# A decoder step in three-pass fp32: the cached keys of the samples scored by products and sums instead of transposes and matmuls

## The reference, cut to what matters

```python
def _dilated_step(q, k, v, buf, window, dil):
    ...
    nk = window // dil + 1                       # 129: 128 cached rows and the sample's own
    g = kv[:, jnp.maximum(cidx, 0)]
    s = jnp.einsum('bthe,btjhe->bthj', q, g[:, :, :, 0])
    lse = jax.nn.logsumexp(s, axis=-1)
    p = jnp.exp(s - lse[..., None])
    o = jnp.einsum('bthj,btjhe->bthe', p, g[:, :, :, 1])
    return o, lse, kv[:, T:]
```

## Time and profile before

| what | value |
|---|---|
| median of 3 runs | 911.78 us (911.31 to 916.65) |
| profiled execution, its own time | 912.07 us |
| its span, first to last instruction | 910.3 us |
| TensorE busy | 900.8 us (99%) |
| VectorE, ScalarE, GpSimd busy | 66%, 54%, 24% |
| bytes moved by DMA | 281.18 MB, mean 309 GB/s |

### The profile page before, as it was taken

The page is one execution under the profiler, slowest core; times in us unless marked ns, Lnnn a source line. Parts: engine busy times, 40 slices in busy tenths (PEclk is TensorE's granted clock), DMA queues, the critical chain, the costliest instruction groups (busy, mean ns, idle before and its releaser), DMA issues.

```text
span 910.3 us, 19532 instructions
## 1 busy us (share of the span) xinstructions
PE 900.8 (99%) x7987; PEld 868.7 (95%) x7987; DVE 601.5 (66%) x868; ACT 488.6 (54%) x753; POOL 216.1 (24%) x233
## 2 busy tenths in 40 slices
PE   8999999999999999999999999999999999999998
PEld 8999999999999999999999999789999999999998
DVE  6666665659975688797887544355548666666543
ACT  6444434445545677677866455246675644443332
POOL 0433330005710000069871113000001043333000
PEclk9999999999999999999999999999999999999999
DMA  9988969999987877789988688849999799998971
GB/s 353 401 309 310 321 227 340 334 356 379 329 306 259 322 255 271 287 316 408 416 316 286 235 267 254 295 163 351 336 367 343 267 352 376 374 364 287 353 221 48
DMA packets 62440, 281.18 MB, mean 309 GB/s; under 512 B 8176, under 2 KB 9328, under 8 KB 60624
## 3 DMA queue, kind: packets, MB, share of 16 engines
q1 hardware_dynamic: 23328, 148.32, 42.9%
q10 hardware_dynamic: 39024, 131.61, 42.5%
HBM read 256.65 MB, written 111.32 MB: 404 GB/s over the span
## 4 chain that ended last, share of the span: by engine, by line
PE 91%; DVE 3%; ACT 2%; DMA 1%; issue 1%; POOL 1%; SPq 0%; ACTq 0%; DVEq 0%; POOLq 0%
PE acc L427 16%; PE acc L428 15%; PE acc L429 15%; PE att L427 11%; PE att L428 10%; PE att L429 10%; PE aux L1063 2%; DVE wl L407 1%; PE att L1188 1%; PE att L1122 1%; DMA kv<-cache 1%; ACT wh L401 1%; PE att L805 1%; PE aux L1027 1%; PE att L1258 1%
## 5 line engine op out<-in xcount | busy, mean ns | idle before, releaser
L407 DVE TENSOR_TENSOR wl<-raw,wh 128x1024 fp32r<-128x1024 f32 (+2 forms) x280 | 334.3, 1196 | 219.5 <-ACT wh L401 214.5
L401 ACT ACTIVATE wh<-raw 128x1024 fp32r<-128x1024 f32 (+2 forms) x280 | 277.0, 994 | 186.8 <-PE acc L429 104.0
L427 PE MATMUL acc<-hh,wh 128*128 128x264 f32 x496 | 145.8, 294 | 0.1
L428 PE MATMUL acc<-hl,wh 128*128 128x264 f32 x496 | 140.8, 284 | 0.0
L429 PE MATMUL acc<-hh,wl 128*128 128x264 f32 x496 | 140.6, 284 | 0.0
L427 PE MATMUL acc<-xh,wh 128*128 128x264 f32 x416 | 118.7, 285 | 1.7 <-DVE wl L407 1.7
L427 PE MATMUL att<-xh,wh 128*128 128x264 f32 x416 | 118.5, 285 | 0.3 <-DVE xl L532 0.3
L428 PE MATMUL acc<-xl,wh 128*128 128x264 f32 x416 | 117.8, 283 | 0.0
L428 PE MATMUL att<-xl,wh 128*128 128x264 f32 x416 | 117.8, 283 | 0.0
L429 PE MATMUL att<-xh,wl 128*128 128x264 f32 x416 | 117.8, 283 | 0.0
L429 PE MATMUL acc<-xh,wl 128*128 128x264 f32 x416 | 117.8, 283 | 0.0
(11 more groups left out here) (264 smaller groups left out, 2075.2 us busy)
## 6 DMA issues: line engine op xcount, KB each, us to landing
raw<-w ACTq DMA_DIRECT2D x207, 512.0 KB, 6.9
state<-state_in SPq DMA_DIRECT2D x32, 512.0 KB, 9.1
state_out<-state SPq DMA_DIRECT2D x32, 512.0 KB, 6.0
raw<-w ACTq DMA_DIRECT2D x32, 384.0 KB, 5.9
kv<-cache SPq DMA_DIRECT2D x48, 256.0 KB, 4.5
raw<-w ACTq DMA_DIRECT2D x32, 320.0 KB, 5.5
raw<-w SPq DMA_DIRECT2D x9, 512.0 KB, 9.0
kv_out<-cache SPq DMA_DIRECT2D x3, 960.0 KB, 7.2
```

Source lines behind the costliest of these rows:

```text
L401: nc.scalar.activation(wh[n % HI_RING][:, 0:slot_size(n)], raw[n % RAW_RING][:, 0:slot_size(n)], ACT.Copy).then_inc(hi_done, 1)
L407: nc.vector.tensor_tensor(wl[n % RAW_RING][:, 0:slot_size(n)], raw[n % RAW_RING][:, 0:slot_size(n)], wh[n % HI_RING][:, 0:slot_size(n)].bi ...
L427: nc.tensor.matmul(out, w_hi, xh, start=first, stop=False)
L428: nc.tensor.matmul(out, w_hi, xl, start=False, stop=False)
```

## The change

The scores of the cached keys leave TensorE. There are now six **items** (two halves of four samples x three groups). An item's keys are loaded as two buffers of 128 partitions x 2 rows x 512, with four cache rows of a sample on each partition. The queries are packed by GpSimd, transposed once by TensorE (`pe_q_rows`, v11), and for each item VectorE spreads its query row over the partitions with a stream shuffle (`dve_key_spread`, 128 x 512 from PSUM). The keys are multiplied by the spread query in place, 128 x 1024 at a time: item 0 on VectorE, items 1 to 5 on GpSimd (`key_product`). VectorE sums each product over the 64 numbers of a head (`dve_key_sum`, 128 x 1024 to 128 x 16). The softmax is made for four samples at a time along the free axis after a VectorE transpose; the three groups are joined by shuffles between partitions. The values come as 12 more buffers in eight loads of 128 KB an item; `pe_dec_v` has the same 24 matmuls of 512 columns, now in slots 9, 11, 16 and 17. Turn, gather and output are done twice, once for each half of the samples. `split_ob` on GpSimd comes after item 1's products, and TensorE waits for its parts one by one in slots 0 and 1. The two transposes of an item of the prompt's attention share one bank.

Elsewhere: slots 0 and 1 of the kernel are rounded in halves, and gate A is read from PSUM with tanh(x/2) in the ga slots, so that the eight sigmoids fall away; the merge becomes (tanh + 1) * A * 0.5 + B in the same two VectorE instructions a tile.

```diff
+        ITEMS = 2 * G
+        ON_POOL = (1, 2, 3, 4, 5)
...
+        def dve_key_spread(dve, i):
+            if i == 0:
+                dve.wait_ge(q_rows, 1)
+            if i >= 2:
+                dve.wait_ge(key_mul, (2, 4, 8, 10)[i - 2])
+            c, g = i // G, i % G
+            nc.vector.stream_shuffle(spread_buffer(i)[:], bank6[:], [2 * g + c] * 32).then_inc(key_spread, 1)
+
+        def key_product(eng, ops, i, half):
+            eng.wait_ge(kv_in[i % 3], kv_landed(i))
+            eng.wait_ge(key_spread, i + 1)
+            if i:
+                eng.wait_ge(key_mul, 2 * i + half)
+            elif half:
+                eng.wait_ge(key_mul, 1)
+            keys = kv_buffer(i, half)
+            ops.tensor_tensor(keys[:], keys[:], spread_buffer(i)[:].unsqueeze(1).to_broadcast([P, 2, AW]),
+                              ALU.mult).then_inc(key_mul, 1)
+
+        def dve_key_sum(dve, i, half):
+            dve.wait_ge(key_mul, 2 * i + half + 1)
...
+            nc.vector.tensor_reduce(to, kv_buffer(i, half)[:].rearrange("p k (h e) -> p k h e", h=AH), AX.X,
+                                    ALU.add).then_inc(key_sum, 1)
...
+        def pe_own_score(pe):
...
+            for t in range(AT):
+                a = 2 * (AT - 1 - t)
+                for j in range(4):
+                    last = nc.tensor.matmul(bank7[32 * j:32 * j + 32, 0:2], head[:, a:a + 32], own_prod[:, t, j:B:4],
+                                            start=t == 0, stop=t == AT - 1)
...
-        DEC_V = {2: (7,), 3: (4, 4), 4: (5,), 5: (5, 5)}
-        OA_SPLIT = {0: (0,), 1: (1,), 3: (2,), 6: (3,)}
+        DEC_TURN = {6: 0, 14: 1}
+        DEC_V = {9: (0, 1), 11: (2,), 16: (3, 4), 17: (5,)}
+        DEC_GATHER = {13: 0, 19: 1}
+        KEY_SPREAD = {-8: 0, -7: 1, -4: 2, -1: 3, 4: 4, 6: 5}
+        KEY_PRODUCT = {-6: (0,), -5: (1,)}
+        KEY_SUM = {-6: (0,), -5: (1,), -3: (2,), -2: (3,), 0: (4,), 1: (5,), 3: (6,), 4: (7,), 6: (8, 9), 8: (10, 11)}
+        SOFT_MAX = {1: 0, 9: 1}
+        SOFT_EXP = {2: 0, 10: 1}
+        SOFT_SUM = {3: 0, 11: 1}
+        OWN_ROWS = {12: 0, 18: 1}
+        DEC_OUT = {13: 0, 19: 1}
+        OA_SPLIT = {4: (0,), 5: (1, 2), 6: (3,)}
...
-                nc.scalar.activation(gate_a[:, t], acc[bank_of(p_ga, t)][:, 0:T], ACT.Copy).then_inc(out_of["act"], 1)
+                nc.scalar.activation(gate_a[:, t], acc[bank_of(p_ga, t)][:, 0:T], ACT.Tanh, scale=0.5).then_inc(out_of["act"], 1)
...
-            for m in range(KD):
-                nc.scalar.activation(gate_a[:, m], gate_a[:, m], ACT.Sigmoid).then_inc(gate_done, 1)
...
-            for h in range(RH):
-                split_ob(h)
+            pool_pad(pool)
+            for i in range(ITEMS):
+                if i == 2:
+                    for h in range(RH):
+                        split_ob(h)
+                for half in range(2):
+                    if i in ON_POOL:
+                        pool_key_product(pool, i, half)
...
+                    if m == 0 and k % 4 == 0:
+                        pe.wait_ge(ob_split, k // 4 + 1)
```

More of the change, by code:

```diff
@@ new lines, in kv_landed, with sp_kv_load @@
+        def kv_landed(n):
+            return sum(32 if m < ITEMS else 128 for m in range(n % 3, n + 1, 3))
+        def sp_kv_load(sp, n):
+            if n >= 3:
+                kv_used(sp, n - 3)
+            c, g = n % ITEMS // G, n % G
+            dil = GROUPS[g][1]
+            for half in range(2):
+                buffer = kv_buffer(n, half)
+                if n < ITEMS:
+                    rows = caches[g][4 * c:4 * c + 4].rearrange("b w c -> (b w) c").rearrange(
+                        "(p k d) c -> p k d c", k=4, d=dil)
+                    sp.dma_start(buffer[:], rows[:, 2 * half:2 * half + 2, 0, 0:AW]).then_inc(kv_in[n % 3], 16)
+                else:
+                    two = caches[g][4 * c + 2 * half:4 * c + 2 * half + 2].rearrange("b (p k d) c -> k p b d c", k=4, d=dil)
+                    for k in range(4):
+                        sp.dma_start(buffer[32 * k:32 * k + 32], two[k, :, :, 0, AW:2 * AW]).then_inc(kv_in[n % 3], 16)
@@ new lines, in pe_dec_v @@
+        def pe_dec_v(pe, i):
+            c, g = i // G, i % G
+            if g == 0:
+                pe.wait_ge(dec_act, 2 * c + 2)
+            n = ITEMS + i
+            pe.wait_ge(kv_in[n % 3], kv_landed(n))
+            for j in range(4):
+                a = 32 * j + AH * g
+                last = nc.tensor.matmul(bank7[32 * j:32 * j + 32, :], dec_pT[:, a:a + 32], kv_buffer(n, j // 2)[:, j % 2],
+                                        start=g == 0, stop=g == G - 1)
+            last.then_inc(dec_v_done, 1)
@@ L1290, in pe_own_score @@
-        def pe_own_score(pe):
-            for g in range(G):
-                for n in range(4):
-                    last = nc.tensor.matmul(bank7[32 * n:32 * n + 16, G * P + g:G * P + g + 1], own_blk[:, 4 * g + n],
-                                            ones[:, 0:1], start=False, stop=g == G - 1, skip_group_check=True)
-            last.then_inc(dec_pe, 1)
-        NK = G * P + G
-        def dve_dec_max(dve):
-            dve.wait_ge(dec_pe, 1)
-            nc.vector.tensor_reduce(dec_m[:, 0:1], bank7[:, 0:NK], AX.X, ALU.max).then_inc(dec_dve, 1)
-            dve.wait_ge(dec_dve, 1)
-            nc.vector.tensor_scalar(dec_m[:, 1:2], dec_m[:, 0:1], -SCALE, None, ALU.mult).then_inc(dec_dve, 1)
@@ L1493, in _ @@
             sp.wait_ge(qk_done, AT)
[L1494 to L1503 removed]
+            for n in range(2 * ITEMS):
+                sp_kv_load(sp, n)
             for q in range(p_pb.q0 + 2, fi2.q0):
@@ L1841, in _ @@
                     dve_v_tile(dve, p_v, AT - V_LAST + t)
-                for i in range(3 * t, 3 * t + 3):
-                    if i % 2:
-                        key_copy(dve, i)
+                dec_steps(t - KD)
                 if t == 1:
```

470 lines of the change are left out of this document (232 added, 238 removed).

## The result

The changed kernel takes 920.5 us (median of 5 runs, 919.5 to 922.9), the kernel before 912.5 in the same comparison: ratio 1.0089, 95% interval 1.0073 to 1.0106. The forecast was 904, with a range of 892 to 914. The profiled execution after has a span of 919.4 us and took 921.22; the one before, 912.07. So there are 9.15 us to explain between the two profiles, and 17 between forecast and profile.

What follows compares the result with a forecast made beforehand. TensorE's own queue was taken as the bound (busy 900.8 of 910.3 us at full clock). From 912.1 us, a gross gain of 20.8 less 13 of stalls gave 904.3, about 904; own range 900 to 908, full range 892 to 914.

Steps and rivals of the forecast that it cites:

- Costs that I put at nothing: Key and value loads and SyncE's delayed cache rolls: a few bunched, covered by ten slots of weights, no cost.
- The clock: TensorE's granted clock might fall in the stalls, making the forecast wrong; no case in the old trace, no size given.
- the stalls: VectorE and GpSimd excluding each other, and VectorE's order, make TensorE wait: 16.0 us laid out, 13 taken, bounds 3 and 16.
- The gross gain: Work off TensorE 18.2, start 1.0, gate 1.2 and small waits 0.4: 20.8 us before stalls.
- The own scores: On TensorE, 96 passes with 32 weight columns and 2 moving ones: 1.6 us added, bounds 1.2 and 2.4.
- The two small changes: First weight tiles in halves gain 1.0 us (bounds 0, 1.6); gate without sigmoids gains 1.2 (bounds 0, 1.3).
- slot 5, for its weights: Item 2's sums, a softmax and blocked low parts make slot 5's weights ready at 572.7, not 571.1: 1.6 us.
- `prob`, first: VectorE reaches the attention's first scores at 582.0, division ends 584.65, TensorE is there at 580.2: 4.5 us lost.
- `prob`, second: Slot 6's spread and two sums stand before the other half's reciprocal on VectorE: 3.4 us lost.
- B: Rival: engines overlap better because GpSimd runs in the gaps; stalls 4 us, time 895 us; chance 0.33.
- C: Rival: GpSimd's in-place product with broadcast input costs 5.2 us, not 2.4, adding 25; time 929 us; chance 0.09.
- D: Rival: stalls reach all 16 us and a few late loads or restarts add to them; time 910 us; chance 0.13.

Runs made afterwards that it cites:

- e1_paced: Changed kernel with SyncE's list of cache rolls begun at slot 12, not slot 8, also called the paced kernel; 909.9 us, ratio to before 0.9967.
- e5_small_packets: Changed kernel with its heap of rolls kept, each roll issued as two transfers in 2 KB pieces; 910.0 us, ratio to before 0.9965.
- e3_no_products: e1_paced with all twelve key products left out, so scores are not the reference's; 896.8 us, ratio to before 0.9821.
- e6_small_two: Kernel before with only the first two weight tiles prepared in halves and the gate by tanh; 911.5 us, ratio 0.9987.
- e7_behind: e1_paced with VectorE's cached-key steps put behind the attention's own steps from slot 5 on; 905.5 us, ratio to before 0.9917.
- e11_sum_later: e9_one_spread_later plus item 1's products on VectorE and TensorE's small retention sum at the end of g0; 904.8 us, ratio to before 0.9920.
- The five arrangements: Five variants of e1_paced moving steps between slots, engines or order, nothing left out; 905.5, 917.2, 906.4, 905.5 and 904.8 us.
- e9_one_spread_later: e7_behind with item 4's spread and item 3's second sum moved from slot 4 to slot 5; 906.4 us, ratio to before 0.9930.
- e2_burst_before: Kernel before with SyncE made to wait for slot 12 before its rolls, so that they heap up; 932.2 us, ratio 1.0210.

## Why the prediction was wrong

**The step that failed** stands under "Costs that I put at nothing": "a few come bunched, under the same cover; if weights land late, TensorE would wait for ScalarE". I had seen that SyncE waits for the value products of slot 11 before it goes on with the rolls, and had named the wait that would follow. I gave it no price, because the bytes were the same and "ten slots of weights cover them". Bytes were not the measure. Behind SyncE's heap the weights move 0.33 to 0.39 MB in each 10 us from 630 to 670, and 0.93 to 1.27 before. It costs 10.6 us (`e1_paced`). No part of that step was worked out: the slots that the rolls wait for, the slot after which SyncE is free, and so the count that leaves at once, could be had from the diff, and the sizes of the packets from the old trace (from 640 to 650 us, 65 packets of 33 KB in SyncE's queue beside 260 of 3.6 KB with weights). The Trainium skill's rule on turns by packet, named under `e5_small_packets`, bears on just this step, and I had not weighed it.

**The clock** was named as a risk without a case. It fell behind the waits for `prob` and for `gate_a`, and cost 5.5 us by the account above; 2.6 of them belong to the rolls. Without the heap the forecast is still short: `e1_paced` takes 909.9 us where 904.3 was forecast, of which some 3 us are the clock and 1.8 the stalls (14.8 for the 13 taken). The range of 892 to 914 would have held it.

**The gross gain** was right in size: 20.8 forecast, 19.4 to 22.3 by the sums under `e3_no_products`. TensorE's busy time there is 884.0 us, 16.8 less than before, inside the 16 to 19 given; in the changed kernel it fell by 10.4 only, with the half clock in it. Single terms were off and made up for each other. The own scores took 0.98 us (1.6 taken, bounds 1.2 and 2.4, so below both). The two small changes gave 0.4 and 0.9 us in `e6_small_two` for 1.0 and 1.2. The first weight pass came at 8.13 us, and not before 7.5 as I had written; 8.46 before; the low part at 25.91 before is at 25.32 now, so the start gave 0.6 here.

```profile
L1283 PE MATMUL aux<-own_prod,tab 128*32 128x2 f32 x96 | 1.0, 173 | 0.0
```

**The stalls** were right too, four of the five one by one:

| place | laid out | measured |
|---|---|---|
| `os_sum` in g0 | 1.4 | 1.3 |
| `obl` in slots 0 and 1 | 5.1 | 4.1 |
| slot 5, for its weights | 1.6 | none; 1.5 at the start of slot 4 (568.22 us), for `gate_b` |
| `prob`, first | 4.5 | 4.4 |
| `prob`, second | 3.4 | 3.5 |
| together | 16.0 | 14.8 |

The third is luck in its size: VectorE was late as laid out, but what TensorE missed first was the accumulator bank that the gate's product frees, one slot before the weights that I had followed. I took 13, a fifth off for meetings that miss; hardly any missed. VectorE and GpSimd side by side, first VectorE, then GpSimd, with the times of one instruction in the second column:

```profile
543.85 2.78 DVE L429 TENSOR_TENSOR wl<-raw,wh 128x1024 fp32r<-128x1024 f32 x1
...
561.49 1.22 DVE L1327 TENSOR_REDUCE scoreT<-kv 128x16 f32<-128x1024 f32 x1 [4.67 <-POOL kv L1309]
...
580.12 0.68 DVE L1155 CUSTOM_DVE_ANT_0 prob<-att,tab 128x512 f32<-128x512 f32 x1
```

```profile
539.79 2.40 POOL L1309 TENSOR_TENSOR kv<-kv,q_wide 128x1024 f32<-128x1024 f32 x1 [7.70 <-DVE kv L1309]
542.36 3.19 POOL L1309 TENSOR_TENSOR kv<-kv,q_wide 128x1024 f32<-128x1024 f32 x1 [0.17 <-POOL kv L1309]
545.51 13.60 POOL L2026 TENSOR_TENSOR obl<-ob,obh 128x1056 fp32r<-128x1056 f32 x4
```

A product takes 2.40 alone and 3.19 behind a low part (3.5 forecast); the low part issued at 543.85, while that product still has 1.7 us to run, takes 2.78 and not 1.2; the four of `split_ob` take 13.60 with low parts between them, 10.1 before. Both bars of a meeting are long: the time of one is in the other's bar. VectorE came to the first scores at 580.1 (582.0 laid out). Each waits for the rest of the other's instruction here too, up to 1.7 us, where the old trace had rows only up to 1.2. The Trainium skill (SBUF — State Buffer, Who interferes with whom) calls the port pair that the two share an exclusive lock, and says that a trn2 `tensor_reduce` never contends for it. The trace agrees, also in that a key sum (561.49) keeps its 1.22 us beside a GpSimd product. Sums of 1.25 and shuffles of 0.7 were forecast; 1.21 and 0.74 came (the rule of 0.14 + 1.04 ns an element gives 542 ns for the row of 554 that it was read from). No table load stands between exp and tanh: ScalarE's loads are one fewer than before, that of the sigmoids.

**The rivals.** B (engines overlap, 895) and C (a product of 5.2 us, 929) both fall by the rows above: stalls 14.8 and not 4, products with a mean of 2.6 and not 5.2. D, that all stalls stand "and a few late loads or restarts add to them", was the nearest in kind, at 910; but it gave those loads under 3 us (912.1 - 20.8 + 16 is 907.3), and the heap made one wait of 8.2. That `e1_paced`, with nearly full stalls and no heap, gives 909.9, D's number, is in part luck: one fall of the clock stands in the place of D's late loads.

**What is better than both kernels.** `e7_behind`, two edits away, takes 905.5 us (0.9917 of before, 0.9897 to 0.9936), and `e11_sum_later` 904.8 (0.9920, 0.9891 to 0.9949); the two cannot be told apart. What is left to `e3_no_products` is 8 to 9 us. I put it down to VectorE, which in the changed kernel is full or waiting for GpSimd (4.67 us in slot 1) from 541 to 582 us. The five arrangements from `e7_behind` to `e11_sum_later` did not get under 904.8 us; whether work can be taken off VectorE there (ScalarE is busy for 4.5 of the 20 us from 560 on) was not tried.

## What to carry to other kernels

When a change makes an issuing engine late, count what it has left to issue at that moment and what those issues were paced by: overdue waits fall through, and a queue that was fed two by two is filled at once. Compare its packets, not its bytes, with those of the queue that must not be late. And when work is handed to a free engine, add up the busy time of the engine that shares its operands in the stretch concerned: over the span VectorE was at 68%, over the 20 us from 560 on at 91%, with the time that it is blocked counted in. The five arrangements left it at 90 to 99% there.

## What the runs showed of the hardware that I had not expected

- Two queues with work on the same 16 DMA engines move packets in equal number when one has large ones: 96 and 97 with 33 and 3.4 KB, 91 and 92 in the kernel before with the same heap. The one with small packets gets a tenth of the bytes. With pieces of 2 KB on the other side it gets 1.04 of 3.6 MB, all that it asks for.
- Small pieces cost no time here, though SyncE was busy issuing them for some 60 us: 105,627 packets instead of 62,630 in the whole kernel, at the same mean of 310 GB/s as the paced kernel, and its time. SyncE's queue took 46.8% of the DMA engines' span for the same bytes, and 43.5% in the paced kernel.
- TensorE's granted clock fell to 0.50 behind the waits of 4.4 and 8.2 us, and the passes then ran 0.22 us apart instead of 0.12. About 3 us went each time beside the wait itself. It fell behind shorter waits too: 0.50 from 584 to 590 us in `e9_one_spread_later`, behind waits of 1.3 and 2.9 us. The waits are not shown to be the whole cause. In `e2_burst_before` it was at 0.50 from 600 to 602 us, far ahead of the heap and with no wait of more than 0.2 us near, where the profile of before has none of it. A stall that is followed by such a stretch is dearer than it is long.
